# GpSimd's sums of weight blocks begin at the end of the first seven-product pair

## The reference, cut to what matters

```
h    = rmsnorm(x)
proj = h @ w_in           # 2048 x 13376: q, k, v, z_attn, z_ssm, x/B/C stream, dt
attn = rmsnorm(dilated_attention(q, k, v)) * silu(z_attn)
ssm  = ssd_branch(z_ssm, xbc, dt)
mix  = concat([attn, ssm]) @ w_out     # 4096 x 2048
y    = x + rmsnorm(mix)
```

## Time and profile before

| | us |
|---|---|
| median of 3 runs | 2439.43 |
| the three runs | 2438.70 to 2440.55 |
| profiled execution, its own time | 2437.86 |
| its span | 2436.1 |
| PE busy | 2405.7 (99% of the span) |
| DVE busy | 1731.5 (71%) |
| ACT busy | 979.3 (40%) |
| POOL busy | 389.5 (16%) |

### The profile page before, as it was taken

One profiled execution on the slowest core, in us unless ns is written; L12 is line 12 of the kernel. 1 busy time (PEld: TensorE's weight loads), 2 busy tenths in 40 slices (PEclk: granted clock), 3 DMA queues, 4 the chain that ended last, 5 costly groups with the idle time before them and its releaser, 6 DMA issues.

```text
span 2436.1 us, 37150 instructions
## 1 busy us (share of the span) xinstructions
PE 2405.7 (99%) x13708; PEld 2284.2 (94%) x13708; DVE 1731.5 (71%) x2435; ACT 979.3 (40%) x1622; POOL 389.5 (16%) x580
## 2 busy tenths in 40 slices
PE   7999999999999999999999999999999999999998
PEld 6999999999999999999999999999999988888887
DVE  5686765555565555564787888788878768787767
ACT  6323433333333333333445444544454533234332
POOL 0000444444444444440000000000000000000000
PEclk9999999999999999999999999999999999999999
DMA  4235455555555555555464546554654435443544
GB/s 162 79 108 162 152 163 155 163 155 158 163 155 166 155 155 155 155 157 199 151 190 143 179 142 188 172 152 142 192 167 133 145 112 180 156 156 121 170 165 159
DMA packets 316776, 379.43 MB, mean 156 GB/s; under 512 B 20006, under 2 KB 237286, under 8 KB 313751
## 3 DMA queue, kind: packets, MB, share of 16 engines
q1 hardware_dynamic: 265063, 222.06, 29.9%
q10 hardware_dynamic: 33200, 106.02, 13.1%
q0 software_dynamic: 18432, 50.36, 6.6%
HBM read 299.16 MB, written 86.54 MB: 158 GB/s over the span
## 4 chain that ended last, share of the span: by engine, by line
PE 85%; DVE 1%; DMA 1%; ACT 1%; issue 0%; ACTq 0%; DVEq 0%; SPq 0%
PE ps L1012 35%; PE ps L810 22%; PE ps L1165 14%; PE ps L1085 4%; PE ps L971 2%; PE ps L938 2%; PE ps L905 2%; PE ps L921 1%; PE ps L981 1%; DMA w_raw<-in_w_in 1%; PE ps L945 0%; PE ps L912 0%; PE ps L954 0%; PE ps L994 0%; PE ps L1207 0%
## 5 line engine op out<-in xcount | busy, mean ns | idle before, releaser
L1012 PE MATMUL ps<-h_hi,w_hi 128*128 128x384 f32 x960 | 322.5, 336 | 0.0
L1012 PE MATMUL ps<-h_lo,w_hi 128*128 128x384 f32 x960 | 322.0, 335 | 0.0
L1012 PE MATMUL ps<-h_hi,w_lo 128*128 128x384 f32 x960 | 321.7, 335 | 0.0
L2194 DVE TENSOR_TENSOR w_lo<-raw_qk,w_hi 128x512 fp32r<-128x512 f32 x240 | 183.3, 764 | 182.7 <-ACT w_hi L1538 181.7
L810 PE MATMUL ps<-h_hi,w_hi 128*128 128x384 f32 x1056 | 275.1, 341 | 0.0
L1245 ACT ACTIVATE w_hi<-w_raw 128x512 fp32r<-128x512 f32 x176 | 109.9, 628 | 400.3 <-PE ps L810 271.2
L810 PE MATMUL ps<-h_lo,w_hi 128*128 128x384 f32 x1056 | 268.9, 335 | 0.0
L810 PE MATMUL ps<-h_hi,w_lo 128*128 128x384 f32 x1056 | 268.8, 335 | 0.0
L1012 PE MATMUL ps<-t_hi,w_hi 128*128 128x384 f32 x720 | 243.4, 338 | 0.9 <-DVE w_lo L2194 0.7
L1012 PE MATMUL ps<-t_hi,w_lo 128*128 128x384 f32 x720 | 243.5, 338 | 0.0
L1012 PE MATMUL ps<-t_lo,w_hi 128*128 128x384 f32 x720 | 242.6, 337 | 0.0
(11 more groups left out here) (327 smaller groups left out, 5183.9 us busy)
## 6 DMA issues: line engine op xcount, KB each, us to landing
raw_qk<-in_w_in SPq DMA_DIRECT2D x90, 512.0 KB, 4.3
w_raw<-in_w_in SPq DMA_DIRECT2D x176, 256.0 KB, 3.6
stage<-loc_scr ACTq DMA_DIRECT2D x16, 1536.0 KB, 7.3
stage<-t_scr SPq DMA_DIRECT2D x48, 512.0 KB, 3.6
stage<-in_w_out POOLq DMA_DIRECT2D x144, 128.0 KB, 2.8
t_scr<-stage POOLq DMA_DIRECT2D x144, 128.0 KB, 2.3
stage<-in_w_out SPq DMA_DIRECT2D x36, 512.0 KB, 3.7
stage<-zx_scr ACTq DMA_DIRECT2D x46, 384.0 KB, 8.9
```

The lines of the kernel that those rows point to most:

```text
L1012: ins = nc.tensor.matmul(ps[:, bank, 0:HALF_T], w, h(k), start=(start and kk == 0 and q == 0), stop=(last and kk == KC - 1 and q == 2), sk ...
L2194: nc.vector.tensor_tensor(w_lo[:, n_slot(n, pp), :], src, w_hi[:, n_slot(n, pp), :].bitcast(f32), ALU.subtract).then_inc(w_lo_done, 1)
```

## The change

POOL's second wait ahead of its first turn is another one. The wait on `cb_stored` stays. POOL now waits for `half_done` of `HP` (14).

```diff
             pool.wait_ge(cb_stored, 16 * SSM_GROUPS)
-            pool.wait_ge(w_lo_done, NC)
+            pool.wait_ge(half_done, HP)
             turns = [(step, k, c) for step in range(BLOCK_STEPS) for k in range(GRP) for c in range(0, HALF_N, SUM_COLS)]
```

## The result

| | before | changed |
|---|---|---|
| median | 2439.23 us (6 runs) | 2450.04 us (6 runs) |
| range | 2436.86 to 2441.09 | 2447.26 to 2454.52 |
| profiled execution, its own time | 2437.86 | 2449.56 |
| its span | 2436.1 | 2447.8 |

The ratio is 1.0045, with a 95% interval of 1.0032 to 1.0058: slower by 10.8 us, outside the predicted range, and on the side that had a chance of 0.06. The same changed kernel was later run 26 times more. These 26 lie between 2435.05 and 2452.82, with a median of 2442.3; all six of the table are at 2447.26 or above, and only five of the 26 are. So the sign is firm, but the size of 10.8 us belongs to the six runs of the table. That this one kernel scatters over 19 us is a part of the story.

A forecast was written before the change was run, and what follows sets the result against it. PE, busy 99% of the span, was taken as the bound. Pair 0's -0.73, pair 1's -1.02 and 0 for the tail sum to -1.75 us: median 2439.43 to 2437.7, 8-in-10 range 2435.3 to 2440.9.

The forecast's parts named there:

- Pairs 0 and 1: PE's stalls in the first two pairs: both go with POOL absent from pair 0, -0.73 and -1.02 us.
- the named chain: Into pair 1: pair 0's last `w_lo` ends 2.27 us sooner, then `raw_d`, DVE's sum and the `w_lo` PE awaits.
- POOL ends near 1127, before 1133.9, at no cost: Tail behind the pairs: POOL's last store lands before SP must issue the k tile's first load; 0 us.
- The deadline: At the k tile: SP may issue its first load as late as 1133.9 without PE waiting.
- One microsecond for each: At SP's wait on `sum_out`: cost per microsecond that POOL's last landing is behind 1133.9.
- Rival 3: At SP's wait on `sum_out`: POOL ends too late for the k tile, slower, 2440.9 or 2452.9; chance 0.12.
- Rivals 1 and 2: In the pairs: only pair 0 gains, 2438.7, chance 0.13; or nothing is gained, 2439.4, chance 0.13.
- rival 1: Pair 1 keeps its stall, `raw_d` late or POOL hitting DVE's block sums; only pair 0's -0.73, 2438.7; chance 0.13.
- The blocking: DVE's `w_lo` beside POOL, stretched up to 1.677 us: returns wherever the turns go, but steady pairs carried it at 29.38 us.

The follow-up runs named there:

- run 26: Not a label but part of "run 26 times more": the changed kernel without edits, 2435.05 to 2452.82 us, median 2442.3.
- changed_look_4: The changed kernel run again without edits, one profiled execution: own time 2452.82 us, with 852.5 us from POOL's first load to its last store.
- changed_third: The changed kernel run again without edits: median 2443.85 us, ratio 1.0018; its profiled execution took 2435.05 us, with 833.0 us for POOL's work.
- wait_at_c3: The changed kernel with SP's three waits on `sum_out` moved from ahead of the k tile's four loads to ahead of the fourth alone: 2440.20 us, ratio 1.0008.

## Why the prediction was wrong

**Pairs 0 and 1: right.** -0.73 and -1.02 us, by the named chain (`raw_d` 2.26 us sooner, 2.27 forecast), in the profiles that started POOL at 14 or later, and with the start at 10.

**"POOL ends near 1127, before 1133.9, at no cost": the step that failed.** Three terms in it:

1. *The length of POOL's work.* Its lower end was 47 x 17.44 + 15.6 less the issue, 835 us, from one execution of the kernel before, and the 1127 that it settled on stands for about 838. Seven executions of the changed kernel gave 833.0 to 852.5, among them the first profile with 850.4 and a mean turn of 17.8 us: 12 us more than was taken. Over 47 turns an error of 2% in a turn is 16 us, while the room was 1133.9 - 1127 = 7. The upper end that the prediction named for the landing, 1137.1, was too low as well: 1141.65 was measured, 2.5 of it because POOL's first load went out at 289.12 and not at 286.6, and 1143.9 in changed_look_4. The range of a sum of 48 rounds was drawn from one sample, with 6 us added for the 1.5 MB loads. The turn beside them took 21.9 us, 4 more than the mean, but four other turns of that trace took 21 us or more, and some 15. In the trace of the kernel before, single turns behind the first took from 14.7 to 21.3 us, which the prediction didn't use.

2. *The deadline.* PE's need of the first k load was placed at 1133.9 for SP's issue; with POOL's first load at 286.6 and 2.1 us of landing this is a total of 845.2, and 844.7 was measured. That was right, and it was the wrong consumer. Behind SP's wait there is also the third load, which hangs on the store of c1, on DVE's addition, and that stands behind the first k load's `w_lo` in DVE's order: 7.2 us. By the table it goes out 850.2 us behind POOL's first load when nothing holds it, at 1136.8 for the forecast's 286.6, so the first must be out by 1129.6. Alone, this error wouldn't have turned the forecast, since 1127 is ahead of 1129.6 too; with the 12 us of the first term it adds some 4 us to the lateness. The stores and loads behind SP's wait stood in the description of the kernel, and the prediction priced only the first.

3. *The price.* "One microsecond for each" holds for the gap at line 810 (0.7 to 27.6 us, to 0.1). Beside changed_third, where POOL was in time, the first profile has the third load 9.5 us later, counted from POOL's first load, and line 921 9.3 us later, where the gap is 5.6. A further 2.0 us lie behind line 921, with the clock at 1.2 GHz for a part of that stretch. Together this is 11.2 us in the last column of the table.

**Rival 3: the mechanism was right, place and sign, and its chance of 0.12 too small.** The prediction had worked out that 34 us of cover met a shift of 38.2, and then let the steady turn decide. Its two figures, 2440.9 and 2452.9, enclose the result, but the upper one was made of other terms (the whole shift and three slow turns) at the price of line 810 alone, so that it came near is luck. Rivals 1 and 2 did not occur at 14; rival 1 was seen at 7.

**The blocking** was weighed rightly. `w_lo`, 0.69 us when clean, took up to 1.78 us beside POOL's turns in the first profile of the changed kernel, and pairs 1 to 28 took 29.38 us each all the same. The rule of the Trainium skill (SBUF — State Buffer, Who interferes with whom), that a VectorE instruction with two inputs in SBUF contends with a GpSimd instruction that reads SBUF, agrees with these rows. Whether a blocked `w_lo` costs the kernel time is read from PE's starts.

## What to carry to other kernels

Work that lies beside the critical path has two edges: before it is started later, list everything that is queued behind the wait for its end, on every engine whose order it crosses, and take the deadline of the earliest consumer, here the third load and not the first. The length of a long train of dependent small transfers is no constant: take it from several executions, and leave a margin of a few per cent of the whole train. And when a kernel's runs scatter by 19 us where its neighbour's scatter by 6 or 7, look for a wait near its threshold.

## What the runs showed of the hardware

POOL's 48 turns of loads, additions and stores, the same instructions each time, took from 833.0 to 854.1 us (the last in wait_at_c3) in 48-turn kernels. What sets this total isn't settled. The granted clock fell behind waits of 2.2 us and more at line 921, and not behind waits of 1.3 to 1.8 us; from that line to the end of the span it is 1262.4 to 1264.0 us in the profiles with the longer waits and 1260.7 to 1261.6 in the others, so a fall costs 1 to 3 us by these sums, as much as the whole gain of the edit. And the code ahead of pair 0, identical in all seven profiles of the changed kernel, let POOL's first load, which follows the end of pair 0, go out anywhere from 285.45 to 289.29. The granted clock between 90 and 100 us explains nearly all of it. Full throughout, it goes with 285.45 and 285.83; a loss of 1.75 us there, with 287.11; losses of 3.4 us, with 288.70 to 289.29. One profile of each kernel would pass such a scatter off as an effect of an edit.
